# First norm in two parts, two feature tiles side by side, and the weight stream reordered in the opening of a two-layer hybrid backbone

## The reference, cut to what matters

```python
mod_l = (silu(c) @ w_mod[l] + b_mod[l])[:, None, :]          # six vectors of 1024, for the latents
mod_c = (silu(c_ctx) @ w_mod[l] + b_mod[l])[None, None, :]   # the same for the context
hl = modulate(rms_norm(x, norm1[l]), sh1, sc1)               # scale and shift by the first two vectors
hc = modulate(rms_norm(xc, norm1[l]), sh1c, sc1c)
zl = split_cols(hl @ w_in[l]); zc = split_cols(hc @ w_in[l])
# branch A: retention, q, k (features), v, g (tokens), decay exp(log_gamma * distance)
# branches B, C, D: gated linear attention, grouped-query attention, differential attention
# then gated merge, output projection, residual, norm, gated MLP with depthwise conv, residual
```

## Time and profile before

| | us |
|---|---|
| median of 3 runs | 2688.01 |
| lowest and highest | 2680.22, 2689.31 |
| span of the profiled execution, first to last instruction | 2687.2 |
| TensorE busy in it | 2569.9 |
| TensorE's mean granted clock, as a share of full | 0.987 |

### The profile page before, as it was taken

The page is one execution under the profiler, slowest core; times in us unless marked ns, Lnnn a source line. Parts: engine busy times, 40 slices in busy tenths (PEclk is TensorE's granted clock), DMA queues, the critical chain, the costliest instruction groups (busy, mean ns, idle before and its releaser), DMA issues.

```text
span 2687.2 us, 37847 instructions
## 1 busy us (share of the span) xinstructions
PE 2569.9 (96%) x15408; PEld 2120.4 (79%) x15408; DVE 1361.2 (51%) x1877; ACT 761.7 (28%) x1276; POOL 1472.2 (55%) x1375
## 2 busy tenths in 40 slices
PE   5999999999999999999999999999998999999999
PEld 2788877877777888888878888786777777888777
DVE  3632266543577777555564562227654677421231
ACT  4611333432355511111120132133522454111200
POOL 3443466522423627666669335447734445688886
PEclk9999999999999999999999999999999999999999
DMA  7422322312313834444434463122221237333322
GB/s 269 150 73 95 110 58 70 83 50 85 87 50 102 267 110 120 117 124 123 117 102 123 124 209 83 52 55 71 79 60 47 71 120 221 110 102 95 93 86 81
DMA packets 378210, 285.10 MB, mean 106 GB/s; under 512 B 10309, under 2 KB 338729, under 8 KB 377526
## 3 DMA queue, kind: packets, MB, share of 16 engines
q1 hardware_dynamic: 375744, 279.81, 35.0%
q10 hardware_dynamic: 1686, 2.78, 0.3%
q0 software_dynamic: 608, 0.09, 0.0%
HBM read 253.28 MB, written 29.36 MB: 105 GB/s over the span
## 4 chain that ended last, share of the span: by engine, by line
PE 82%; DVE 10%; ACT 3%; POOL 2%; issue 1%; DMA 1%; ACTq 0%; DVEq 0%; SPq 0%; POOLq 0%
PE ps L532 19%; PE ps L533 18%; PE ps L534 18%; PE ps L1194 3%; PE ps L738 3%; PE ps L576 2%; PE ps L577 2%; PE ps L578 2%; PE ps L822 2%; DVE ffl L2472 2%; PE ps L947 2%; PE ps L842 2%; POOL w_lo L1348 1%; PE ps L1143 1%; POOL w_hi L1345 1%
## 5 line engine op out<-in xcount | busy, mean ns | idle before, releaser
L1345 POOL TENSOR_TENSOR w_hi<-ring,tiny 128x512 fp32r<-128x512 f32 x480 | 535.3, 1115 | 988.6 <-PE ps L534 580.5
L532 PE MATMUL ps<-hh,w_hi 128*128 128x512 f32 (+1 forms) x2320 | 847.8, 365 | 11.6 <-DVE hl L2030 10.4
L1348 POOL TENSOR_TENSOR w_lo<-ring,w_hi 128x512 fp32r<-128x512 f32 (+1 forms) x568 | 797.8, 1407 | 82.2 <-ACT w_hi L1551 44.5
L533 PE MATMUL ps<-hl,w_hi 128*128 128x512 f32 (+1 forms) x2320 | 820.7, 354 | 0.0
L534 PE MATMUL ps<-hh,w_lo 128*128 128x512 f32 (+1 forms) x2320 | 820.2, 354 | 0.0
L532 PEld LDWEIGHTS ps<-hh,w_hi 128*128 128x128 f32 x2320 | 442.8, 191 | 107.7 <-issue 27.8
L534 PEld LDWEIGHTS ps<-hh,w_lo 128*128 128x128 f32 x2320 | 442.4, 191 | 61.8
L533 PEld LDWEIGHTS ps<-hl,w_hi 128*128 128x128 f32 x2320 | 443.8, 191 | 55.5 <-issue 1.0
L1670 ACT ACTIVATE arena<-ps,tiny,vec 128x768 f32<-128x768 f32 (+1 forms) x120 | 108.6, 906 | 187.4 <-DVE tiny L2207 187.3
L1842 ACT ACTIVATE arena<-ps,vec 128x768 f32<-128x768 f32 (+1 forms) x44 | 39.0, 887 | 426.1 <-PE ps L534 426.1
L2481 DVE SCALAR_TENSOR_TENSOR arena<-ps,vec,arena 128x511 f32<-128x511 f32 x66 | 43.6, 661 | 221.7 <-ACT arena L1842 220.9
(11 more groups left out here) (271 smaller groups left out, 3825.5 us busy)
## 6 DMA issues: line engine op xcount, KB each, us to landing
ring<-in_w_in SPq DMA_DIRECT2D x118, 512.0 KB, 4.0
ring<-in_w_mod SPq DMA_DIRECT2D x96, 512.0 KB, 3.9
ring<-in_w_up SPq DMA_DIRECT2D x88, 512.0 KB, 4.2
ring<-in_w_down SPq DMA_DIRECT2D x48, 512.0 KB, 3.7
ring<-in_w_out SPq DMA_DIRECT2D x32, 512.0 KB, 3.8
logits<-arena SPq DMA_DIRECT2D x32, 384.0 KB, 2.5
arena<-logits SPq DMA_DIRECT2D x32, 384.0 KB, 4.2
ring<-in_w_down SPq DMA_DIRECT2D x24, 384.0 KB, 3.2
```

What stands on the lines that cost most here:

```text
L532: pe.matmul(acc, wh[:, offset + k], hi[:, n, x:y], start=n == 0, stop=False)
L533: pe.matmul(acc, wh[:, offset + k], lo[:, n, x:y], start=False, stop=False)
L1345: pool.tensor_tensor(wh[:, 0:count], w, one[:].unsqueeze(2).to_broadcast([P, count, P]), ALU.mult).then_inc(*up("w_lead", ("lead", key, j)))
L1348: pool.tensor_tensor(wl[:, 0:count], w, wh[:, 0:count].bitcast(F32), ALU.subtract).then_inc(*up("w_split", ("split", key, j)))
```

## The change

Four things are done together, all in layer 0.

1. `PARTS[0, 1]` splits the first norm: ScalarE and VectorE go over all 8 channel tiles for the 512 latents first and then over all 8 for the 256 context tokens. ScalarE takes the raw `x` tiles out only during the second pass (`tokens_again(k - 2)` behind `hh[k]` of the context, the last two behind the loop).
2. `opening_projections` computes feature tiles 0 and 1 together: for each k the three products of tile 0 and of tile 1 over the latents, and after all 8, the same over the context with `turn_tokens("x", k)` behind each k. Both tiles become full at the end. The conditioning chunks that stood behind tile 0 and tile 1 now come together after both.
3. In the weight stream both feature tiles stand ahead of conditioning group 3: chunks 12 and 13 instead of 16 and 19. `dist` and `rope` are issued behind the last chunk of group 3.
4. The `xn` turns are moved among the conditioning chunks: none before the end of group 0, then behind (0,3), (1,0), (1,2), (1,3), (2,1), (2,3), (3,1), (3,3). ScalarE takes out group 0 before `xn` 0.

```diff
+PARTS = {(0, 1): {"first": (0, LAT), "second": (LAT, T)},
...
+        for g in range(4) if l == 0 else ():
+            order += ([("f", l, "ret", n) for n in OPENING] if g == 3 else []) + [("msl", l, g, kk) for kk in range(4)]
...
-                order += [("f", l, b, n)] + slices_behind(l, b, j)
+                order += ([] if opens(l, b, n) else [("f", l, b, n)]) + slices_behind(l, b, j)
...
+            def opening_projections(keys):
+
+                for n, key in enumerate(keys):
+                    next_chunk(key)
+                    for s, c in room(key, 2 * n, 2 * n + 1):
+                        pe.wait_ge(s, c)
+                for part, (x, y) in PARTS[0, 1].items():
+                    for k in range(KT):
+                        j = k // (KT // 2)
+                        pe.wait_ge(*at(("hl", 0, 1, part, k)))
+                        for key in keys:
+                            if part == "first" and k % (KT // 2) == 0:
+                                pe.wait_ge(*at(("split", key, j)))
+                            mm = product(psum(key)[:, x:y], key, j, hh, hl, x, y, count=1, first=k, offset=k % (KT // 2))
+                            if part == "second" and k % (KT // 2) == KT // 2 - 1:
+                                mm.then_inc(*up("pe_half", ("half", key, j), *([("full", key)] if j else [])))
+                        if part == "second":
+                            turn_tokens("x", k)
...
-                            if kk % 2 == 1:
-                                turn_tokens("xn", 2 * g + kk // 2)
+                            for k in {(0, 3): (0,), (1, 0): (1,), (1, 2): (2,), (1, 3): (3,), (2, 1): (4,), (2, 3): (5,),
+                                      (3, 1): (6,), (3, 3): (7,)}.get((g, kk), ()):
+                                turn_tokens("xn", k)
...
-                if key == ("f", 0, "ret", 0):
+                if key == ("msl", 0, 3, 3):
                     sp.dma_start(*loads[2]).then_inc(*up("dist_in", ("dist_in",), by=16))
-                if key == ("f", 0, "ret", 1):
                     sp.dma_start(*loads[1]).then_inc(*up("rope_in", ("rope_in", 0), by=16))
...
-                    tokens_out("xn", xn, 0)
                     act.wait_ge(*at(("free", ("vec", 0))))
-                    for g in range(4):
+                    modulation_columns(0)
+                    tokens_out("xn", xn, 0)
+                    for g in range(1, 4):
+                        tokens_out("xn", xn, 2 * g)
                         modulation_columns(g)
...
+                    for s, (part, (x, y)) in enumerate(PARTS[0, 1].items()):
+                        for k in range(KT):
+                            act.activation(hh[:, k, x:y], xn[:, k, x:y], ACT.Identity, scale=a1[:, 0, k, s:s + 1],
+                                           bias=modv[:, k, s:s + 1]).then_inc(*up("lead_ready", ("hh", l, which, part, k)))
+                            if part == "second" and k >= 2:
+                                tokens_again(k - 2)
+                    tokens_again(KT - 2)
                     tokens_again(KT - 1)
...
+                        for k in range(KT):
+                            if k >= 2:
+                                dve.wait_ge(*at(("hl", l, which, part, k - 2)))
+                            dve.tensor_scalar(tb_first[:, k % 2, x:y], xn[:, k, x:y], a1[:, 0, k, s:s + 1], modv[:, k, s:s + 1],
+                                              ALU.mult, ALU.add).then_inc(*up("scaled", ("scaled", l, which, part, k)))
+                            if k >= 1:
+                                dve.wait_ge(*at(("scaled", l, which, part, k - 1)))
+                                rest_of(k - 1)
+                        dve.wait_ge(*at(("scaled", l, which, part, KT - 1)))
+                        rest_of(KT - 1)
```

More of the change, by code:

```diff
@@ L94, in constants @@
     return dict(k_small=small, k_rope=rope, k_dist=dist, k_mask=mask.reshape(P, -1))
-PARTS = {(1, 1): {"first": (0, LAT), "second": (LAT, T)},
+PARTS = {(0, 1): {"first": (0, LAT), "second": (LAT, T)},
+         (1, 1): {"first": (0, LAT), "second": (LAT, T)},
          (0, 2): {"first": (0, LAT), "second": (LAT, T)},
@@ L207, in steps_of, with opens @@
     return {"ret": 4, "gla": 8, "gqa": 4, "dif": 4}[b] * NQ[l] if b != "after" else 1
+OPENING = (0, 1)
+def opens(l, b, n):
+    return l == 0 and b == "ret" and n in OPENING
 def weight_chunks():
@@ L508, in _ @@
         def _(pe):
-            tenant, used, turn = {}, [0], [0]
+            tenant, taken, turn = {}, set(), [0]
             def room(key, *banks):
@@ L519, in next_chunk @@
             def next_chunk(key):
[L520 to L523, removed]
+                assert key in place and key not in taken, key
+                taken.add(key)
             def product(acc, key, j, hi, lo, x, y, count=KT // 2, first=0, whole=KT, each=None, offset=0):
@@ L1052, in _ @@
                             each = None
-                            if b == "ret" and j == 0:
-                                each = lambda k: ("hl", l, 1, "first", k) if l else ("hl", l, 1, k)
+                            if b == "ret" and j == 0 and l > 0:
+                                each = lambda k: ("hl", l, 1, "first", k)
                             if b == "ret" and j == BR[b]["nq"] and l > 0:
@@ L1210, in _ @@
                 mm.then_inc(*up("pe_full", ("full", ("final", t))))
-            assert used[0] == len(chunks)
+            assert len(taken) == sum(key[0] != "slice" for key in chunks)
         @block.sync
@@ L1489, in tokens_again @@
             def tokens_again(k):
-                act.wait_ge(*at(("scaled", 0, 1, k)))
-                act.wait_ge(*at(("hh", 0, 1, k)))
+                act.wait_ge(*at(("scaled", 0, 1, "second", k)))
+                act.wait_ge(*at(("hh", 0, 1, "second", k)))
                 tokens_out("x", xT, k)
@@ L1504, in norm @@
                             decays()
[L1505 to L1508, removed]
+                        modulation_bias(g - 1)
                     modulation_bias(3)
                     act.wait_ge(*at(("scale_set", 1)))
[L1511 to L1517, removed]
+                    for s, (part, (x, y)) in enumerate(PARTS[0, 1].items()):
[5 more added lines that the diff above has]
+                    tokens_again(KT - 2)
                     tokens_again(KT - 1)
@@ L2026, in norm, with rest_of @@
                         dve.wait_ge(*at(("free", ("xn", k))))
[L2028 to L2036, removed]
-                            ins = dve.tensor_scalar(tb_first[:, k % 2, x:y], xn[:, k, x:y], a1[:, 0, k, s:s + 1], modv[:, k, s:s + 1],
-                                                    ALU.mult, ALU.add)
-                        ins.then_inc(*up("scaled", ("scaled", l, which, k)))
-                        dve.wait_ge(*at(("scaled", l, which, k)))
-                        rest_of(k)
+                    for s, (part, (x, y)) in enumerate(PARTS[0, 1].items()):
+                        def rest_of(k):
+                            dve.wait_ge(*at(("hh", l, which, part, k)))
+                            dve.tensor_tensor(hl[:, k, x:y], tb_first[:, k % 2, x:y], hh[:, k, x:y].bitcast(F32), ALU.subtract).then_inc(
+                                *up("rest_ready", ("hl", l, which, part, k)))
+                        for k in range(KT):
[8 more added lines that the diff above has]
+                        rest_of(KT - 1)
                     return
```

12 lines of the change are left out of this document (7 added, 5 removed).

## The result

Over 7 runs of each the changed kernel took 2698.40 us (2691.97 to 2699.65) and the kernel before 2688.01 (2680.22 to 2693.87): a ratio of 1.0033, 95% interval 1.0021 to 1.0045, so it is slower by 6 to 12 us. The forecast was 2699, slower.

What follows compares the result with a forecast made beforehand. The prediction took TensorE, busy 96% of the span, as the bound, with its wait on ScalarE's serial chain. 2687.2 + 5.6 (chain head) + 2.5 (rounds) + 3.1 (clock) = 2698.4, so 2699 as median; range 2688 to 2706.

Steps and rivals of the forecast that it cites:

- The bound and the chain: From ScalarE's copy of feature 0 at 80.31 to the first token pair at 114.16, a 33.85 us chain without TensorE.
- Tiles issued at 36.2 and 36.7: Weight stream: chunks 12 and 13, feature tiles 0 and 1, issued then and landed at about 40.0 and 41.4.
- The splits in series in front of chunk 17: Last chunk of group 3 waits for two GpSimd splits of 4.7 us, lands at 53.2, 5.1 later than before.
- The first hh at 57.9: ScalarE's first `hh` of the norm comes at 57.9 instead of 53.62, VectorE's scale saving 0.8.
- The upper bound of +5.5: Largest delay allowed for ScalarE's first `hh`, if `dist` and `rope` slow chunk 17 by 1.4.
- The opening's products: TensorE's two feature tiles and eight turns: start at 59.7, 22.0 at full clock plus 3.1 for half clock.
- the head of the chain: ScalarE starts to take out feature 0 at 85.9 instead of 80.31, +5.6 us.
- The rounds: VectorE's first two strip rounds, beside GpSimd's splits, grow from 14.0 to 16.5 together: +2.5, bounds -2.2 and +5.5.
- Tile 2's late weights: TensorE waits about 5 us for feature tile 2's split, hidden under the chain and costing nothing by itself.
- The clock behind the longer wait: TensorE's longer wait before the first token pair brings half clock again: +3.1, between 0 and 3.1.
- The faster one: Rival, chance 0.08: TensorE's own stream sets the first token pair's start, 4.9 earlier, and 2679 would be reached.
- The no-change one: Rival, chance 0.34: opening nearly as early, chunk 17 there at 50.7, feature 0 copied at 80.3; 2685 to 2691 us.

Runs made afterwards that it cites:

- the weights alone: Kernel before with only the weight order changed: both feature tiles ahead of conditioning group 3, `dist` and `rope` behind it; 2695.07 us, ratio 1.0025.
- the tiles amid group 3: Changed kernel with both feature tiles between the second and third chunk of conditioning group 3 in the weight stream; 2689.94 us, ratio 1.0010.
- TensorE kept busy: Changed kernel plus nine unread TensorE products around the chunks and the turning of conditioning group 3; 2689.93 us, ratio 1.0010.
- short splits: Changed kernel, GpSimd splitting only 16 of 128 columns for feature tiles 2 and 3 and the first token pair; 2694.83 us, ratio 1.0029.
- the copy first: Changed kernel with ScalarE's copy of feature 3 ahead of its exponentials of strip 2; 2695.74 us, ratio 1.0033.
- the turns alone: Kernel before with only the `xn` turns moved among the conditioning chunks and group 0 taken out ahead of `xn` 0; 2685.60 us, ratio 0.9995.

## Why the prediction was right, point by point

**The bound and the chain.** Right. Where the chain begins and what it passes through are the same before and after, and putting strip 2's exponentials, 3.4 us, behind the copy of feature 3 moved the pair by 3.0.

**Tiles issued at 36.2 and 36.7, landed at 40.0 and 41.4.** Issued at 35.30 and 39.34; GpSimd begins at 41.57. The second tile was 2.6 late since chunk (2,1), whose place it takes, was multiplied only at 37.38, after waiting for its landing, and took 1.92 us at half clock.

**The splits in series in front of chunk 17.** Right in mechanism and nearly in size: split until 49.4 forecast, 51.0 measured, chunk multiplied at 53.2 forecast, 55.27 measured. The runs with the weights alone and with the tiles amid group 3 show that it is mostly this wait, some 5 us, and that the two transfers take some 3 more.

**The first hh at 57.9.** It came at 62.94, so +9.3 instead of +4.3: the step that failed. Of the 5.0, 2.1 are the later chunk and 3.0 the stretch behind it. The forecast took that stretch as before, less 0.8, 4.7 us; it was 7.67. TensorE had waited 3.9 us for the last chunk and was at half clock for all of that stretch, and 1.85 us of turning became 3.41. With TensorE kept busy the stretch was 4.6. The upper bound of +5.5 is a small slip too: 4.3 + 1.4 is 5.7, still far below 9.3. The forecast looked for half clock only behind the pause in front of the norm.

**The opening's products.** Start 1.86 us behind the first `hh`, 1.8 forecast; 22.0 + 3.1 forecast, 23.4 measured (64.80 to 88.2). Part of the half clock had been spent ahead of it. Copy 0 at 89.06, forecast 85.9: **+8.75 at the head of the chain instead of +5.6.**

**The rounds.** 14.3 before (7.8 and 6.55), 17.5 after: +3.2, forecast +2.5; in the second profile 10.1 and 5.5, only +1.3. The short splits show the cause. The first round is even longer than the 9.7 us that the prediction named as the worse case; the second had fewer splits beside it.

**Tile 2's late weights.** Wait of 6.1, forecast 5; hidden under the chain, as forecast. It is not free once the chain is shortened: with the copy first the remaining wait of 3.1 is ScalarE's copy behind TensorE's own late end.

**The clock behind the longer wait.** It did fall, and cost 1.4 (13.3 - 11.9), not 3.1: it fell at 122.3, while TensorE was still waiting, and was at full again at 129.1, 3 us behind the pair's start. That the wait of 3.4 left the clock at full in the kernel before was luck of its one profile: behind the same wait of 3.35 with the turns alone it was at half from 112.0 to 115.4, and behind one of 3.1 with the weights alone from 123.3 to 126.8.

**The sum.** Forecast 5.6 + 2.5 + 3.1 = 11.2; measured in the profile 8.75 + 3.2 + 1.4 = 13.3, of which 3.3 came back behind the opening. So the near agreement of 2699 with 2698.4 is partly luck: a head 3.1 too small and rounds 0.7 too small, against a clock term 1.7 too large and 3.3 us from dips of the clock behind the opening. The same kernel run again came to 2695.82, 8.0 above the kernel before beside it, where the first difference is 10.4.

**The rivals.** The faster one needed the chain cut; it was not. The no-change one needed the last chunk by 50.7; with the tiles two chunks later in the list (weights amid) it comes at 49.24, and the time is 1.0010. In its sum the prediction takes 2.5 off copy 0, where its own bound, chunks 1.8 sooner, allows 1.8: 81.0 and not 80.3.

**What stays open.** The medians are closer to each other than the profiles' openings: the changed kernel without its weight order has a pair 5.1 us later than before, and a time only 1 us longer; the kept-busy run a pair 11.2 later and 1 us. One profile of each kernel can't say how the half-clock stretches of the opening fall in the mean. The two profiles of the changed kernel differ by 1.1 at the first `hh` and 2.4 at copy 0. For the kept-busy kernel the runs show one thing more: its mean granted clock over all eleven is 0.9895, against 0.9871 for the kernel before beside it, so part of the 11 us may have come back as clock elsewhere. That it did, and why, no run shows.

## What to carry to other kernels

When a load is moved forward in a ring of buffers, look at which later load reuses its place, and at what frees it: places freed by slow two-step splits in front of the critical load cost some 5 us here, and moving the same loads by two positions gave most of it back. Ask which consumer's first piece of work begins a serial chain on another engine: finishing two tiles together moved the first one back (copy 0 at 82.53 with the old weight order, at 78.22 with the turns alone), and the chain hung on the first. Where a wait covers several buffers, take each wait only where its buffer is first written: that shortened one wait by 1.5 us here. And before a difference of some us between two profiles is explained, take a second profile of one of them.

## What was not expected of the hardware

TensorE's granted clock fell to half while it was waiting for single chunks with 1 us of work between them, not only in a long pause: in the changed kernel at 37.0, 47.2 and 54.1. The small products behind the last chunk then took nearly twice their time: 1.85 us before, 3.41 in three of the four profiles of the changed kernel's opening and 1.99 in the fourth, and 1.85 with TensorE kept busy. In the first 140 us of the kernel before the granted clock was at half once; in every profile of the others it was so two to six times. GpSimd's splits and VectorE's strips lengthened each other: a split of 1.27 us took 2.0 and a strip instruction of 1.09 took 1.8 to 2.05.
